# Rotary angle table on GpSimd ahead of the first norm, and the modulation GEMV in pieces beside the last feed-forward

## What is computed

```python
for i in range(2):
    x = x + 0.5 * swiglu(rms_norm(x, ffn1_norm[i]), ...)     # D_FF = 2816
    h = rms_norm(x, mix_norm[i])
    x = x + (moba_mixer(h, positions, ...) if i == 0 else mamba2_mixer(h, ...))
    x = x + 0.5 * swiglu(rms_norm(x, ffn2_norm[i]), ...)
# rotary tables of the attention: ang = positions * 10000 ** (-arange(64) / 64); cos(ang), sin(ang)

mod = silu(c) @ w_ada + b_ada                 # (1, 1024) @ (1024, 3072): 12.6 MB of weights
shift, scale, gate = split(mod, 3)
h = rms_norm_2(x, norm_g) * (1 + scale) + shift
...                                           # projections, HGRN2 and retention
x = rms_norm_2(x + gate * (m @ w_out), final_g)
```

## Time and profile before

| | |
|---|---|
| launches timed (3) | 1507.41, 1508.14, 1509.86 us; median 1508.14 |
| the profiled execution | span 1503.2 us from first to last instruction; its own launch time is not among the three, and what lies around a span is taken as 1508.14 - 1503.2 = 4.9 us |
| TensorE busy | 1402.7 us, 93% |
| VectorE busy | 963.2 us, 64% |
| ScalarE busy | 704.9 us, 47% |
| GpSimd busy | 327.9 us, 22% |
| mean granted TensorE clock | 0.972 |
| DMA | 250.04 MB, 166 GB/s over the span |

### The profile page before, as it was taken

One profiled execution on the slowest core, in us unless ns is written; L12 is line 12 of the kernel. 1 busy time (PEld: TensorE's weight loads), 2 busy tenths in 40 slices (PEclk: granted clock), 3 DMA queues, 4 the chain that ended last, 5 costly groups with the idle time before them and its releaser, 6 DMA issues.

```text
span 1503.2 us, 18620 instructions
## 1 busy us (share of the span) xinstructions
PE 1402.7 (93%) x7153; PEld 1179.5 (78%) x7153; DVE 963.2 (64%) x934; ACT 704.9 (47%) x814; POOL 327.9 (22%) x197
## 2 busy tenths in 40 slices
PE   6629899988999999999989999999999899999996
PEld 5517688867888888888879987788888699888785
DVE  5999954876654456554558788765554557667476
ACT  5303333654544435444456666744444455447343
POOL 3999700331000000000000025300000102326540
PEclk9959999999999999999999999999999999999999
DMA  9735554532555555566545452266555445444240
GB/s 306 257 112 209 180 189 162 171 137 85 172 192 191 192 177 177 187 195 195 174 134 169 144 161 92 85 212 214 187 194 191 156 156 172 151 153 144 89 160 32
DMA packets 157658, 250.04 MB, mean 166 GB/s; under 512 B 8640, under 2 KB 99072, under 8 KB 156448
## 3 DMA queue, kind: packets, MB, share of 16 engines
q1 hardware_dynamic: 155104, 232.94, 47.1%
q0 software_dynamic: 1792, 13.86, 2.7%
q10 hardware_dynamic: 704, 2.44, 0.5%
HBM read 248.16 MB, written 1.05 MB: 166 GB/s over the span
## 4 chain that ended last, share of the span: by engine, by line
PE 82%; DVE 10%; issue 4%; ACT 2%; DMA 1%; POOL 1%; SPq 0%; DVEq 0%; POOLq 0%; ACTq 0%
PE psum L595 9%; PE psum L597 9%; PE psum L596 9%; PE psum L634 4%; PE psum L636 4%; PE psum L635 4%; PE psum L1720 3%; PE psum L451 3%; PE psum L1722 3%; PE psum L1721 3%; PE psum L452 3%; PE psum L453 3%; DVE w_lo L392 3%; PE psum L430 2%; PE psum L432 2%
## 5 line engine op out<-in xcount | busy, mean ns | idle before, releaser
L392 DVE TENSOR_TENSOR w_lo<-raw,w_hi 128x2048 fp32r<-128x2048 f32 x220 | 569.5, 2593 | 330.0 <-ACT w_hi L384 329.8
L384 ACT ACTIVATE w_hi<-raw 128x2048 fp32r<-128x2048 f32 x220 | 421.3, 1916 | 395.4 <-PE psum L597 126.4
L595 PE MATMUL psum<-w_hi,hT_hi 128*128 128x512 f32 x704 | 280.8, 399 | 11.3 <-DVE w_lo L392 5.8
L597 PE MATMUL psum<-w_hi,hT_lo 128*128 128x512 f32 x704 | 276.2, 392 | 0.0
L596 PE MATMUL psum<-w_lo,hT_hi 128*128 128x512 f32 x704 | 276.2, 392 | 0.0
L503 POOL TENSOR_TENSOR meansq<-sumsq 128x2 f32<-128x2 f32 x7 | 4.2, 593 | 740.8 <-ACT xn L474 740.8
L595 PEld LDWEIGHTS psum<-w_hi,hT_hi 128*128 128x128 f32 x704 | 133.5, 190 | 40.2 <-DVE w_lo L392 7.0
L597 PEld LDWEIGHTS psum<-w_hi,hT_lo 128*128 128x128 f32 x704 | 133.3, 189 | 28.7
L596 PEld LDWEIGHTS psum<-w_lo,hT_hi 128*128 128x128 f32 x704 | 133.5, 190 | 26.6
L634 PE MATMUL psum<-w_hi,hidT_hi 128*128 128x512 f32 x320 | 125.2, 391 | 4.3 <-DVE hidT_lo L718 4.1
L636 PE MATMUL psum<-w_hi,hidT_lo 128*128 128x512 f32 x320 | 124.7, 390 | 0.0
(11 more groups left out here) (364 smaller groups left out, 2309.5 us busy)
## 6 DMA issues: line engine op xcount, KB each, us to landing
raw<-in_ffn_w_gate SPq DMA_DIRECT2D x88, 512.0 KB, 4.0
raw<-in_ffn_w_up SPq DMA_DIRECT2D x88, 512.0 KB, 5.0
raw<-in_ffn_w_down SPq DMA_DIRECT2D x88, 512.0 KB, 4.3
raw<-in_w_in SPq DMA_DIRECT2D x72, 512.0 KB, 4.6
raw<-in_ssm_w_in SPq DMA_DIRECT2D x48, 512.0 KB, 4.6
ada_in<-in_w_ada POOLq DMA_DIRECT2D x8, 1536.0 KB, 7.1
raw<-in_attn_w_qkv SPq DMA_DIRECT2D x24, 512.0 KB, 4.6
raw<-in_ssm_w_out SPq DMA_DIRECT2D x16, 512.0 KB, 4.5
```

The lines of the kernel that those rows point to most:

```text
L384: act.activation(w_hi[:, slot, :], raw[:, slot, :], ACT.Copy).then_inc(sem("hi_ready"), 1)
L392: dve.tensor_tensor(w_lo[:, slot, :], raw[:, slot, :], w_hi[:, slot, :].bitcast(F32), ALU.subtract)\
L595: pe.matmul(to, a, hi[:, kk, :], start=k == 0, stop=False)
L597: m = pe.matmul(to, b, hi[:, kk, :], start=False, stop=k == KD - 1)
```

## The change

The angle table leaves VectorE. `angles_pool` makes it on GpSimd, ahead of the first norm, in 18 instructions: a fused multiply and add becomes two instructions, and so does the double limit; products with a column of positions are written with a second operation (times 1). `ada_pool` moves behind the norm of the last feed-forward. Each product and sum is issued as three instructions of 1024 columns, the product with a second operation (times 1.0); the second load is issued at once. Its buffers move to zones of the second block. The sum over partitions is parted: `gate2_pe` stands ahead of the last down products of ffn2_1, `mod_pe` at the head of `second_pe`, and the turned x of the second block's norm leaves bank 3 to it.

```diff
--- before.py
+++ after.py
@@ -231,10 +231,6 @@
         angle = start("angle", [P, 2, TT, HALF])
         turns = start("turns", [P, 2, TT, HALF])
         trig = start("trig", [P, 2, TT, HALF])
-        ada_in = start("ada_in", [P, 2, 3 * D])
-        ada_term = start("ada_term", [P, 3 * D])
-        ada = start("ada", [P, 3 * D])
-        b_ada = start("b_ada", [1, 3 * D])
 
         norm, _ = region(WORK)
         xn = norm("xn", [P, TT, D])
@@ -315,6 +311,10 @@
         def zoned(zone, name, shape, dt=F32, offset=0):
             return at(second[zone] + offset, name, shape, dt)[0]
 
+        ada_in = zoned("pair", "ada_in", [P, 2, 3 * D])
+        ada_term = zoned("sum", "ada_term", [P, 3 * D])
+        ada = zoned("sum", "ada", [P, 3 * D], offset=12 * D)
+        b_ada = zoned("ret_v", "b_ada", [1, 3 * D])
         h_tmp = zoned("pair", "h_tmp", [P, KD, SEQ])
         hg_exp = zoned("exp", "hg_exp", [P, HEADS, SEQ])
         hg_pair = zoned("pair", "hg_pair", [P, HEADS, SEQ])
@@ -458,7 +458,7 @@
 
         def turned_x_bank(n, k):
 
-            return ((4, 5, 6, 7) if n == 2 else (2, 3, 4, 6))[k // 2]
+            return {2: (4, 5, 6, 7), 6: (2, 4, 6, 7)}.get(n, (2, 3, 4, 6))[k // 2]
 
         def turned_x(n, k):
             return psum[:, turned_x_bank(n, k), (k % 2) * SEQ:(k % 2 + 1) * SEQ]
@@ -701,7 +701,7 @@
             turned(NFC - 1, last_hidT_hi)
             split_hi(act, u0 + 3 * NFC - 2 + SLOTS)
 
-        def ffn_dve(dve, f, after_second=None, before_last=None):
+        def ffn_dve(dve, f, before_last=None):
 
             u0 = FIRST_UNIT[f]
 
@@ -727,8 +727,6 @@
             split_lo(dve, u0 + 3 + SLOTS)
             split_lo(dve, u0 + 4 + SLOTS)
             turned(1)
-            if after_second:
-                after_second(dve)
             with dve.Fori(2, NFC - 1) as c:
                 split_lo(dve, u0 + 5 + SLOTS, c - 2, 3)
                 times_up(c)
@@ -777,29 +775,53 @@
                            allow_slow_non_contiguous=True).then_inc(sem("pos_in"), 16)
             pool.dma_start(gains[:, 0, :], w["attn_q_norm"][0].partition_broadcast(P)).then_inc(sem("pos_in"), 16)
             pool.dma_start(gains[:, 1, :], w["attn_k_norm"][0].partition_broadcast(P)).then_inc(sem("pos_in"), 16)
-            pool.dma_start(b_ada[:, :], w["b_ada_2"]).then_inc(sem("b_ada_in"), 16)
             pool.wait_ge(sem("neg_half"), 1)
+
+        def angles_pool(pool):
+
+            order = in_order(pool, "gpsimd_order")
+            pool.wait_ge(sem("pos_in"), 48)
+            pool.wait_ge(sem("const1_in"), 16)
+            order(pool.tensor_copy(pos_f[:, :], pos_i[:, :]))
+            order(*(pool.tensor_scalar(angle[:, a, t, :], c1("freq"), pos_f[:, t:t + 1], 1.0, ALU.mult, ALU.mult)
+                    for a in range(2) for t in range(TT)))
+            order(pool.tensor_scalar(turns[:, 0, :, :], angle[:, 0, :, :], 1 / (2 * np.pi), 0.0, ALU.mult, ALU.add),
+                  pool.tensor_scalar(turns[:, 1, :, :], angle[:, 1, :, :], 1 / (2 * np.pi), 0.25, ALU.mult, ALU.add))
+            order(pool.tensor_scalar(turns[:, :, :, :], turns[:, :, :, :], ROUND, None, ALU.add))
+            order(pool.tensor_scalar(turns[:, :, :, :], turns[:, :, :, :], ROUND, None, ALU.subtract))
+            for part in (TWO_PI_HI, TWO_PI_MID, TWO_PI_LO):
+                order(pool.tensor_scalar(trig[:, :, :, :], turns[:, :, :, :], -part, 0.0, ALU.mult, ALU.add))
+                order(pool.tensor_tensor(angle[:, :, :, :], trig[:, :, :, :], angle[:, :, :, :], ALU.add))
+            order(pool.tensor_scalar(angle[:, 1, :, :], angle[:, 1, :, :], np.pi / 2, 0.0, ALU.add, ALU.add))
+            limit = 3.1415925
+            order(pool.tensor_scalar(angle[:, :, :, :], angle[:, :, :, :], -limit, None, ALU.max))
+            pool.tensor_scalar(angle[:, :, :, :], angle[:, :, :, :], limit, None, ALU.min)\
+                .then_inc(sem("angles"), 1)
+
+        ADA_PIECE = D
 
         def ada_pool(pool):
 
             src = w["w_ada_2"][0].rearrange("(k p) n -> p k n", p=P)
             order = in_order(pool, "gpsimd_order")
+            pieces = [slice(a, a + ADA_PIECE) for a in range(0, 3 * D, ADA_PIECE)]
 
             def load(k):
                 pool.dma_start(ada_in[:, k % 2, :], src[:, k, :]).then_inc(sem(f"ada_in_{k % 2}"), 16)
 
             load(0)
+            load(1)
+            pool.dma_start(b_ada[:, :], w["b_ada_2"]).then_inc(sem("b_ada_in"), 16)
             pool.wait_ge(sem("silu_c"), 1)
             for k in range(KD):
                 pool.wait_ge(sem(f"ada_in_{k % 2}"), 16 * (k // 2 + 1))
-                if k == 0:
-                    load(1)
                 to = ada if k == 0 else ada_term
-                order(pool.tensor_scalar(to[:, :], ada_in[:, k % 2, :], silu_c[:, k:k + 1], None, ALU.mult))
+                order(*(pool.tensor_scalar(to[:, cs], ada_in[:, k % 2, cs], silu_c[:, k:k + 1], 1.0,
+                                           ALU.mult, ALU.mult) for cs in pieces))
                 if k + 2 < KD:
                     load(k + 2)
                 if k:
-                    order(pool.tensor_tensor(ada[:, :], ada[:, :], ada_term[:, :], ALU.add))
+                    order(*(pool.tensor_tensor(ada[:, cs], ada[:, cs], ada_term[:, cs], ALU.add) for cs in pieces))
             pool.wait_ge(sem("b_ada_in"), 16)
             pool.tensor_tensor(ada[0:1, :], ada[0:1, :], b_ada[:, :], ALU.add).then_inc(sem("ada"), 1)
 
@@ -858,26 +880,6 @@
             dve.tensor_copy(taps[:, :], psum[:, 5, P:2 * P]).then_inc(sem("cols"), 1)
             split_lo(dve, 2)
 
-        def angles_dve(dve):
-
-            order = in_order(dve, "vector_order")
-            dve.wait_ge(sem("pos_in"), 48)
-            order(dve.tensor_copy(pos_f[:, :], pos_i[:, :]))
-            for t in range(TT):
-                order(dve.tensor_scalar(angle[:, 0, t, :], c1("freq"), pos_f[:, t:t + 1], None, ALU.mult))
-            order(dve.tensor_copy(angle[:, 1, :, :], angle[:, 0, :, :]))
-            order(dve.tensor_scalar(turns[:, 0, :, :], angle[:, 0, :, :], 1 / (2 * np.pi), None, ALU.mult),
-                  dve.tensor_scalar(turns[:, 1, :, :], angle[:, 1, :, :], 1 / (2 * np.pi), 0.25, ALU.mult, ALU.add))
-            order(dve.tensor_scalar(turns[:, :, :, :], turns[:, :, :, :], ROUND, None, ALU.add))
-            order(dve.tensor_scalar(turns[:, :, :, :], turns[:, :, :, :], ROUND, None, ALU.subtract))
-            for part in (TWO_PI_HI, TWO_PI_MID, TWO_PI_LO):
-                order(dve.scalar_tensor_tensor(angle[:, :, :, :], turns[:, :, :, :], -part, angle[:, :, :, :],
-                                               ALU.mult, ALU.add))
-            order(dve.tensor_scalar(angle[:, 1, :, :], angle[:, 1, :, :], np.pi / 2, None, ALU.add))
-            limit = 3.1415925
-            dve.tensor_scalar(angle[:, :, :, :], angle[:, :, :, :], -limit, limit, ALU.max, ALU.min)\
-               .then_inc(sem("angles"), 1)
-
         def rope_tables_dve(dve):
             dve.wait_ge(sem("trig"), 1)
             sin, cos = trig[:, 0, :, :], trig[:, 1, :, :]
@@ -888,18 +890,25 @@
                        .then_inc(sem("rope_tables"), 1)
 
 
-        def ada_pe(pe):
+        def gate2_pe(pe):
             pe.wait_ge(sem("ada"), 1)
             for h in range(2):
-                pe.matmul(psum[:, h, :], ones, ada[:, 2 * D + 512 * h:2 * D + 512 * (h + 1)], start=True, stop=True)
+                m = pe.matmul(psum[:, h, :], ones, ada[:, 2 * D + 512 * h:2 * D + 512 * (h + 1)],
+                              start=True, stop=True)
+            m.then_inc(sem("mod_ready"), 1)
+
+        def gate2_dve(dve):
+            dve.wait_ge(sem("mod_ready"), 1)
+            dve.tensor_copy(gate2[:, :].rearrange("p (a n) -> p a n", a=2), psum[:, 0:2, :])\
+               .then_inc(sem("mod_read"), 1)
+
+        def mod_pe(pe):
             for j in range(2 * KD):
                 m = pe.matmul(psum[:, 3, j:j + 1], ada[:, j * P:(j + 1) * P], ones[:, 0:1], start=True, stop=True)
             m.then_inc(sem("mod_ready"), 1)
 
-        def ada_dve(dve):
-            dve.wait_ge(sem("mod_ready"), 1)
-            dve.tensor_copy(gate2[:, :].rearrange("p (a n) -> p a n", a=2), psum[:, 0:2, :])\
-               .then_inc(sem("mod_read"), 1)
+        def mod_dve(dve):
+            dve.wait_ge(sem("mod_ready"), 2)
             dve.tensor_copy(mod_cols[:, :], psum[:, 3, 0:2 * KD]).then_inc(sem("mod_read"), 1)
             dve.wait_ge(sem("mod_read"), 2)
 
@@ -942,7 +951,6 @@
                                       for k, src in halves_of(name, k0, 512 * n)])
 
         def attn_pe(pe):
-            pe.wait_ge(sem("mod_read"), 2)
             norm_pe(pe, 1, True)
             u = FIRST_UNIT["qkv"]
             for c in range(6):
@@ -1701,6 +1709,8 @@
             sp.wait_ge(sem("stored"), 16 * TT)
 
         def second_pe(pe):
+            mod_pe(pe)
+            pe.wait_ge(sem("mod_read"), 1)
             norm_pe(pe, 6, False, TT)
             u = FIRST_UNIT["in2"]
```

(12 more changed lines are left out.)

## The result

Device time fell from a median of 1508.18 us (4 launches, 1507.41 to 1509.86) to 1449.57 us (4 launches, 1449.21 to 1450.52): a ratio of 0.961, 95% interval 0.9596 to 0.9624. The forecast was 1452, range 1447 to 1474.

The account below looks back on a forecast made before the run. TensorE works 93% of the span but is held up by VectorE, which takes turns with long GpSimd instructions. 60.2 - 2 - 1.9 = 56.3 us less: span 1446.9, with 4.9 around it 1452 us, range 1447 to 1474.

Parts of the forecast that it names:

- The 60.2 us: How much longer ffn1_0 takes than ffn2_1, first hid to last addition; all of it was to leave ffn1_0.
- The table's price in front, 2 us: Angle table on GpSimd ahead of the first norm: rstd at 35.5 us, about 2 us late for TensorE.
- The one-operation price: Cost of a one-operation product on GpSimd: fixed 0.19 us plus 2.6 ns per column.
- The deadline of 33.8 us: Start of the kernel: the latest time at which rstd can come without TensorE waiting for hid.
- The GEMV's work: GpSimd's work for the GEMV beside ffn2_1: 110 us, done at 1176 with VectorE's turns, 15 us in time.
- A sum piece at 2.35 us: GEMV in ffn2_1: a sum of 1024 columns on GpSimd, priced at 0.19 us plus 2.1 ns per column.
- A product piece at 1.94: GEMV in ffn2_1: a two-operation product of 1024 columns on GpSimd, 0.19 us plus 1.7 ns per column.
- The toll of 1.4 us for each w_lo: Time each VectorE w_lo takes from GpSimd's GEMV in ffn2_1; 42 us for 30, bounds 0.4 and 2.29 each.
- "I charge nothing": ffn2_1: VectorE's w_lo wait for at most one piece, under 3 us, which is covered, so cost nothing.
- Rival 3: ffn2_1: turns don't pass between pieces, VectorE waits for three at once; 2.8 us per block, 1472 us; chance 0.05.
- The sums over partitions: On TensorE: the gate's cost 1.88 us in ffn2_1; shift and scale's 3.63 us hide before the second block's norm.
- Around the span: Time outside the profiled span that is added to reach the launch time, taken as 4.9 us.

Follow-up runs that it names:

- e2: The change with the angle table back on VectorE behind chunk 1, so only the GEMV is moved and cut; 1449.86 us, ratio 0.96.
- e12: Kernel of before, nothing moved: GEMV in pieces of 1024 columns, two-operation products, a wait after each sum piece; 1467.07 us, ratio 0.9727.
- e1: Kernel of before with only the angle table moved to GpSimd ahead of the first norm, GEMV left in ffn1_0; 1480.34 us, ratio 0.9796.
- e8: The change with a wait after each piece of a sum on GpSimd; 1446.89 us, ratio 0.9592.
- e4: The change with GEMV pieces of 3072 columns, each product and sum one instruction; 1454.59 us, ratio 0.9659.
- e3: The change with the GEMV's product pieces in one operation instead of two; 1450.14 us, ratio 0.9626.
- e6: Kernel of before with a second operation (times 1.0) in the GEMV's product of 3072 columns; 1486.41 us, ratio 0.9855.
- e7: The change with the GEMV's second load issued behind the first product; median 1452.77 us, ratio 0.9614.
- e9: The change with the second load behind the first product and a wait after each sum piece; 1446.42 us, ratio 0.9594.
- e5: The change with GEMV pieces of 512 columns; 1454.36 us, ratio 0.9633.
- e11: The change itself, unedited, run once more; 1450.52 us, ratio 0.9611.
- e10: Kernel of before with the table on GpSimd ahead of the first norm; GEMV in ffn1_0, cut, two-operation products, waited sums; 1449.74 us, ratio 0.9608.

## Why the prediction was right

- **The 60.2 us.** Right: 60.6 us left, and for the reason given. Long GpSimd instructions held VectorE's, and the table paid for it as a chain. e2 shows the chain at 4.0 us beside a quiet GpSimd, e12 at 17 us beside pieces, before it was 46. The prediction did not say that either move alone brings the table's part; e1 and e2 show it.
- **What the 60.2 us were made of.** 39.0 us of TensorE's wait at the table, 9.5 of its later waits, 5.5 of sums, and some 3 that the prediction does not name. In the long wait the granted clock fell to 0.50 (1.2 GHz), and it stayed there until about 109.6, 6.2 us after TensorE's work began again at 103.39; at half speed that is 3 us, an estimate. Windows of TensorE before (stretch, length, busy time and count, granted clock, share of the DMA engines in use, GB/s):

```profile
105.00:110.00 5.00, 5.00 (x14) 0.54 0.86 315
110.00:115.00 5.00, 5.00 (x24) 1.00 0.36 108
```

- **The table's price in front, 2 us.** It was nothing. Rstd came 2.6 us earlier than summed. Three two-operation instructions on 256 columns at 0.41 and not 0.63 us are 0.7 of that. Most of the rest is w_lo: the five instructions that met one (1.14, 1.15, 2.01, 2.82 and 2.58 us in the timeline) were held up by 7.7 us in all, an estimate from the same forms undisturbed, where 9.1 were summed. The one-operation price (0.19 + 256 x 2.6 ns = 0.85; measured 0.85 to 0.89) was right. The deadline of 33.8 us was met at 32.86, so TensorE had no wait.
- **The GEMV's work.** A sum piece at 2.35 us was right (2.37). A product piece at 1.94 was too dear: 1.11 us. The term mis-sized is the price per column, from two rows of 2 and 16 columns: 1.7 ns, measured 0.9. That is on the safe side. The toll of 1.4 us for each w_lo was too low in the steady rounds. There a round is 17.55 us (1017.16 to 1034.71), with 3.33 + 7.12 + 1.1 of work: 2.0 us for each w_lo. The GEMV took 133 us against 152, and was 37 us early against 15.
- **"I charge nothing" for VectorE and the loads** is the step that failed: 5.1 us. Its ground was that the turn passes at each instruction, as in the earlier trace rows. In four rounds it did not, and the last three of them cost 2.3 us (e8, with waits, is without them). The bias, one instruction of 6.7 us that the prediction listed as work but not as a thing to wait for, held a w_lo for 6.2 us and cost 0.9. About 2 us are the loads at the start of ffn2_1, 412 to 419 GB/s in 970 to 980, where the prediction had looked at the mean only. One row of the windows of the change shows it (busy time of PE, PEld, DVE, ACT and POOL with their counts, then as above; TensorE works 3.88 of 5 us):

```profile
970.00:975.00 5.00, 3.88 (x18) 2.87 (x16) 3.09 (x1) 4.63 (x4) 4.68 (x5) 1.00 1.05 419
```

- **Rival 3** (turns don't pass between pieces) thus was partly true, at 0.8 us a round where it was priced at 2.8. The price was wrong too: in e4, where every sum is one instruction, the stage is 9.0 us above 175.9, 2.0 of them present with pieces as well, which leaves 1.0 for each of 7 rounds. Why a chunk hides most of a 7 us wait was not tested; cheap products are not needed for it, since e3 has them dear and the same stage. The rule in "Who interferes with whom" of SBUF — State Buffer (the Trainium skill) says that whoever issues first has the shared ports for the whole instruction. These traces agree for sums (each w_lo that waited for one ended 2.15 us behind a piece's end, nearly its whole 2.29) and show more: the holder can keep its turn over three instructions that stand back to back.
- **The sums over partitions:** 1.7 to 1.9 and nothing, as forecast.
- **Around the span** 1.8 us and not 4.9. Two errors met: 3.1 us too much here, and 1.0 too little in the span (1446.9 against 1447.9), so that 1452 stood 2.4 above the result.
- **Luck in the total.** The span came out within 1.0 us because errors met: ffn1_0 gave 2.3 us more than summed (60.6 against 60.2 less 2), the stretch between 1.5 (it varies by as much between runs, 756.9 to 758.5), and the last feed-forward took 4.9 more than the 1.9 charged. The mechanism was right; the last microseconds were not foreseen.

## What to carry to other kernels

Where two engines take turns at a shared resource, the length of one instruction on the slower engine is what each small instruction on the other pays. Keep chains of small dependent instructions away from long ones, or cut the long ones and put a wait between the pieces. Ask also what stands beside them: next to the chunks' large instructions cut and waits were worth 7.1 us in a whole stage, while for the table's chain they took 34 us (e6, second operation only) down to 17 (e12). Cost both forms of an operation from wide rows before ruling on a schedule: one extra operation made GpSimd's product with a column 2.8 times faster. Ask whether a step must move at all; here a cut in place (with the small table elsewhere) gave the same time as the move.

## What the runs showed of the hardware

**One operation is slower than two.** On GpSimd a product with a column as its scalar takes 8.13 us over 3072 columns with one operation and 2.86 us with a second one (times 1.0), in e6. The table shows it with a constant as scalar too, 0.89 (an addition) to 0.41 (a product and an addition) over 256 columns. A sum of two inputs costs 6.66 in both kernels.

**A turn can be kept.** VectorE kept it over two w_lo in a row and GpSimd over three sums; in other rounds it passed at once. VectorE's case, beside the w_lo of e8's first fence: the product's first piece was issued at 1017.16 and ended at 1022.34, 0.92 us behind the end of the second w_lo at 1021.42. In the change a w_lo waited for all three pieces when it came 0.3 to 1.0 us after the first had begun, and for one at 1.2 us. That is no rule: in e3, with the same sums, one came 1.51 us after the first piece (1050.02) and waited for three, and one came 0.82 us after it (1090.23) and waited for one.

```profile
1051.53 7.77 DVE L392 TENSOR_TENSOR w_lo<-raw,w_hi 128x2048 fp32r<-128x2048 f32 x1 [2.03 <-ACT w_hi L384]
...
1091.05 3.73 DVE L392 TENSOR_TENSOR w_lo<-raw,w_hi 128x2048 fp32r<-128x2048 f32 x1 [3.02 <-ACT w_hi L384]
```

With a wait between the pieces (e8, e9) no w_lo waited for more than one. What decides it without the wait was not found.

**Eight microseconds that come and go.** Some launches of one and the same kernel are 8 us longer. The profiled ones show where: in the second block, behind a wait of 1 us for the scan's states, TensorE's granted clock falls from 1.00 (2.4 GHz) to 0.50 (1.2 GHz) for some 20 us, from about 1344.3 to 1364.8 in e7. The windows of TensorE in e7, then the same place in the change, where the clock stayed after the same wait:

```profile
1341.13:1344.13 3.00, 2.08 (x11) 1.00 0.54 207
1344.13:1347.13 3.00, 3.00 (x11) 0.53 0.15 13
1356.13:1359.13 3.00, 3.00 (x16) 0.50 0.00 0
1362.13:1365.13 3.00, 3.00 (x8) 0.56 0.00 0
1365.13:1368.13 3.00, 3.00 (x14) 1.00 0.00 0
```

```profile
1347.09:1350.09 3.00, 2.33 (x13) 1.00 0.45 173
1350.09:1353.09 3.00, 3.00 (x17) 1.00 0.17 14
```

The second block lasted 313.7 us in the profiles of e7, e9, e5, e11 and 313.5 in e1, against 305.6 to 306.3 in the others. Judged by the times of launches, it came in one of ten of the change, three of four of e7, two of five of e9, none of five of e10. It does not need the change: e1, with the GEMV in its old place and the second block as before, has it. It is twice the size of the last improvement, so those were compared by stage. Whether the phase of the work decides it stays open.
